# Two-layer mixer: the second layer's first two projection groups take activations before the norm

## The reference, cut to what matters

```python
shift, scale, gate = split(silu(c) @ w_ada + b_ada, 3)
h = x * rsqrt(mean(x * x) + eps) * norm_gain * (1 + scale) + shift
proj = h @ w_in                 # q, k, v, z of the attention, then q, k, v, z of the retention
```

## Time and profile before

| what | value |
|---|---|
| median of 3 runs | 1535.81 us (1535.54 to 1535.85) |
| time of the profiled execution | 1534.71 us |
| its span in the trace | 1533.0 us |
| TensorE busy, share of the span | 99% |
| DVE busy, share of the span | 74% |
| ACT busy, share of the span | 51% |
| mean granted TensorE clock | 0.997 |

### The profile page before, as it was taken

The page is one execution under the profiler, slowest core; times in us unless marked ns, Lnnn a source line. Parts: engine busy times, 40 slices in busy tenths (PEclk is TensorE's granted clock), DMA queues, the critical chain, the costliest instruction groups (busy, mean ns, idle before and its releaser), DMA issues.

```text
span 1533.0 us, 32039 instructions
## 1 busy us (share of the span) xinstructions
PE 1520.6 (99%) x12566; PEld 1480.7 (97%) x12566; DVE 1134.8 (74%) x1371; ACT 778.1 (51%) x930; POOL 35.4 (2%) x64
## 2 busy tenths in 40 slices
PE   9999999999999999999999999999999999999997
PEld 8999998999999999999999999999999989999997
DVE  7877777658988878878788887879854644764754
ACT  7645456545554445444444444445554643454544
POOL 0000001000000000000000000000000000000000
PEclk9999999999999999999999999999999999999998
DMA  9574566457876867767677776866475554455451
GB/s 351 168 272 159 203 191 246 155 173 265 311 291 239 299 222 274 260 237 285 238 272 240 260 272 223 297 228 210 147 251 194 193 192 165 154 162 179 164 180 56
DMA packets 86412, 340.31 MB, mean 222 GB/s; under 512 B 9896, under 2 KB 10424, under 8 KB 79808
## 3 DMA queue, kind: packets, MB, share of 16 engines
q1 hardware_dynamic: 77760, 281.05, 52.9%
q0 software_dynamic: 7712, 55.63, 10.2%
q10 hardware_dynamic: 864, 2.53, 0.4%
HBM read 337.03 MB, written 2.14 MB: 221 GB/s over the span
## 4 chain that ended last, share of the span: by engine, by line
PE 94%; DVE 4%; ACT 1%; issue 1%; DMA 0%; SPq 0%; DVEq 0%; ACTq 0%
PE PS L1328 27%; PE PS L1330 27%; PE PS L1332 27%; PE PS L1377 3%; PE PS L1376 3%; PE PS L1374 3%; DVE wlo L696 1%; PE PS L1523 1%; PE PS L1544 1%; ACT whi L333 1%; DVE conv_acc L777 1%; DMA raw<-weights 0%; PE PS L1701 0%; PE PS L1506 0%; DVE EM L881 0%
## 5 line engine op out<-in xcount | busy, mean ns | idle before, releaser
L696 DVE TENSOR_TENSOR wlo<-raw,whi 128x1024 fp32r<-128x1024 f32 x528 | 642.8, 1222 | 337.0 <-ACT whi L333 333.6
L333 ACT ACTIVATE whi<-raw 128x1024 fp32r<-128x1024 f32 x528 | 557.4, 1059 | 640.2 <-PE PS L1332 571.0
L1328 PE MATMUL PS<-gh,whi 128*128 128x256 f32 x3096 | 863.4, 279 | 0.7 <-DVE wlo L696 0.4
L1330 PE MATMUL PS<-gl,whi 128*128 128x256 f32 x3096 | 856.1, 277 | 0.0
L1332 PE MATMUL PS<-gh,wlo 128*128 128x256 f32 x3096 | 856.1, 277 | 0.0
L1328 PEld LDWEIGHTS PS<-gh,whi 128*128 128x128 f32 x3096 | 581.7, 188 | 5.6 <-issue 2.4
L1330 PEld LDWEIGHTS PS<-gl,whi 128*128 128x128 f32 x3096 | 581.4, 188 | 0.8
L1332 PEld LDWEIGHTS PS<-gh,wlo 128*128 128x128 f32 x3096 | 581.6, 188 | 0.0
L1328 PE MATMUL PS<-ah,whi 128*128 128x256 f32 x688 | 189.9, 276 | 0.0
L1330 PE MATMUL PS<-al,whi 128*128 128x256 f32 x688 | 189.9, 276 | 0.0
L1332 PE MATMUL PS<-ah,wlo 128*128 128x256 f32 x688 | 189.9, 276 | 0.0
(11 more groups left out here) (254 smaller groups left out, 892.9 us busy)
## 6 DMA issues: line engine op xcount, KB each, us to landing
raw<-weights SPq DMA_DIRECT2D x528, 512.0 KB, 3.5
ada_w<-w_ada POOLq DMA_DIRECT2D x48, 1024.0 KB, 6.5
EM<-rows POOLq DMA_DIRECT2D x1, 3072.0 KB, 12.4
X<-xT SPq DMA_DIRECT2D x3, 512.0 KB, 8.2
c<-const ACTq DMA_DIRECT2D x1, 1536.0 KB, 6.9
c_act<-c_rows POOLq DMA_DIRECT2D x1, 1024.0 KB, 6.7
KF<-factors POOLq DMA_DIRECT2D x2, 512.0 KB, 6.6
outT<-X SPq DMA_DIRECT2D x2, 512.0 KB, 3.2
```

The costliest lines, as they stand in the source:

```text
L333: act.activation(whi[:, j % SPLIT, :], raw[:, j, :], ACT.Copy).then_inc(s_hi, 1)
L696: dve.tensor_tensor(wlo[:, j % SPLIT, :], raw[:, j, :], whi[:, j % SPLIT, :].bitcast(F32), ALU.subtract).then_inc(s_lo, 1)
L1328: pe.matmul(out[:, t, :], whi[:, b, w], hi[:, kt, :], start=first and half == 0 and (apart or t % 2 == 0), stop=False, skip_group_check=True)
L1330: pe.matmul(out[:, t, :], whi[:, b, w], lo[:, kt, :], start=False, stop=False, skip_group_check=True)
```

## The change

Groups 0 and 1 of the second layer's input projection (the columns of z of the attention) take `gh`/`gl` made of X times gain and scale alone, without the norm factor and without the shift. The factor, one number for each position, is multiplied in by DVE when the two accumulators are emptied (`gate_scaled`), and the shift's part, `shift @ w_in` for these 1024 columns, is added as the bias of the silu. From group 2 on the projection takes the normed and shifted activations, which replace the first ones in `gh`/`gl` during group 1. The group d = 3 becomes an ordinary one; `last_pair`, `column_squares`, the spread and `idle` stay only at the end of the kernel (`last_pair`, `column_squares`) and in the first layer. The sum of squares is taken with `sum_squares` (one matmul with ones, in TensorE's slot 5), its root on ACT and its inverse on DVE in their slots 5.

The shift's part is made by DVE during `ffn`: after iteration 2 it adds the bias to the 16 sums, POOL writes them to memory and reads them back onto every partition (`s_rowb`), and in iterations 3 to 10 DVE multiplies this row with one row block of the transposed weights (`w_rowb`, 1 MB, loaded from ACT's queue) and sums it up. Iteration 2 is written out too.

```diff
         @block.gpsimd
-            with pool.Fori(1, ADA_TILES // 2) as i:
...
+            modulation_rows(1, 9)
+            pool.wait_ge(s_shift, 1)
+            pool.dma_start(shift, shift_col).then_inc(s_shiftd, 16)
+            pool.wait_ge(s_shiftd, 16)
+            pool.dma_start(s_rowb[:, :], shift.rearrange("p t -> (p t)").unsqueeze(0).to_broadcast([P, D])
+                           ).then_inc(s_shiftb, 16)
+            modulation_rows(9, ADA_TILES // 2)
...
         @block.scalar   (in ffn, at its top)
+                if i is not first and i is not second:
+                    act.wait_ge(s_wsum, i - 2)
+                    act.dma_start(w_rowb[:, :], w_shift[bass.ds(i - 3, 1), :, :].rearrange("a p n -> (a p) n")
+                                  ).then_inc(s_wrow, 16)
...
             for d in range(4):
+                split(B_IN2 - 1, LEAD + 2 * d)
+                split(B_IN2 - 1, LEAD + 2 * d + 1)
+                act.wait_ge(s_evac, G_IN2 - 4 + d + 3)
+                if d == 0:
+                    act.wait_ge(s_mt, 1)
+                if d < 2:
+                    squares(2, d, SQX2)
+                for t in range(4 * d, 4 * d + 4):
+                    early_hi(t)               # gh[t] = X[t] * modT[16 + t]
             def slot2(n):
+                if n in (0, 2):
+                    squares(2, 2 + n // 2, SQX2)
+                if n == 5:
+                    root(2, D)
+                if n == 8:
+                    act.wait_ge(s_wsum, 1 + 8)
+                    act.dma_start(c2[:, :, :, :], const2).then_inc(s_c2, 16)
+                if 9 <= n < 9 + DT // 2:
+                    late_hi(2 * (n - 9))
+                    late_hi(2 * (n - 9) + 1)
+                if n in (17, 18):             # silu with bias=shift_out[:, t], tile by tile
...
         @block.vector   (in ffn, third block)
+                    if j == 0 and i is not first and i is not second:
+                        shift_product(i)      # waits s_wrow; w_rowb *= s_rowb, summed into small[280 + i - 3]
                     taps = 0 if i is last else 2
...
             ffn(first)
-            with dve.Fori(2, last) as i:
+            ffn(second)
+            dve.wait_ge(s_ada, 16)
+            dve.tensor_tensor(shift_col, modT[:, 0:16], col("b_ada", 0, 16), ALU.add).then_inc(s_shift, 1)
+            dve.wait_ge(s_shiftb, 16)
+            with dve.Fori(3, last) as i:
...
+            for d in range(4):
                 split(B_IN2 - 1, LEAD + 2 * d)
                 split(B_IN2 - 1, LEAD + 2 * d + 1)
                 add_to_x(8 * (B_IN2 - 1) + 2 * d + 1, G_IN2 - 4 + d, (G_IN2 - 4 + d) % 2, 4 * d)
+                if d == 0:
+                    dve.wait_ge(s_mt, 1)
+                if d < 2:
+                    for t in range(4 * d, 4 * d + 4):
+                        early_lo(t)           # gl[t] = X[t] * modT[16 + t] - gh[t]
+                if d == 2:
+                    sum_chunk(2, 1, SQX2)
             def slot2(n):
+                if n < 4:
+                    early_lo(8 + 2 * n)
+                    early_lo(8 + 2 * n + 1)
+                if n in (1, 3):
+                    sum_chunk(2, 2 + n // 2, SQX2)
+                if n == 3:
+                    fold(2, 3, SQX2)
+                if n == 5:
+                    inverse_root(2)
+                    dve.wait_ge(s_rb, 3)
+                if n in (7, 15):
+                    gate_scaled(n // 8)
+                if 6 <= n < 6 + DT // 2:
+                    normed(2 * (n - 6))       # TH[t] = X[t] * modT[16 + t] * rb
+                    normed(2 * (n - 6) + 1)
+                if 9 <= n < 9 + DT // 2:
+                    late_lo(2 * (n - 9))      # gl[t] = TH[t] + modT[t] - gh[t]
+                    late_lo(2 * (n - 9) + 1)
...
             for n in range(IN2_SLOTS):
-                if n >= len(TURNS) - 2:
-                    split(B_IN2, LEAD + n)
+                split(B_IN2, LEAD + n)
                 slot2(n)
...
         @block.tensor
-            last_pair(2, range(4), True, 8 * B_IN2 - 2, ah2, al2)
-            column_squares(2, SQX2)
             def slot2(n):
-                if n == 6:
-                    idle(2)
+                if n == 5:
+                    sum_squares(2, SQX2)      # waits for fold(2, 3)
...
+            need = {0: lambda kt: early + kt + 1, 2: lambda kt: late + kt + 1}
```

More of the change, by code:

```diff
@@ L177, in build, with near_tile @@
         own = PS[:, 4:8, 0:S]
[L178 to L190, removed]
+        rcol = small[:, 228:230]
+        SQUARES, SUMS = (0, 4, 8, 12), (0, 3, 6, 9)
+        late_par = (G_OUT2 + 3) % 2
+        last_spread = PS[:, 2 * late_par + 1, 0:S]
+        shift_col, shift_out = small[:, 288:304], small[:, 280:288]
+        def near_tile(t):
+            return SQX4[:, 1, t, :]
         def seen(h, c):
@@ L307, in _, with modulation_rows @@
                 pool.dma_start(ada_w[:, b, :], w_ada[b, :, :]).then_inc(s_adaw[b], 16)
[L308 to L312 removed]
+            def modulation_rows(first, end):
+                with pool.Fori(first, end) as i:
+                    for b in range(2):
+                        pool.wait_ge(s_ada, i * 2 + (b - 1))
+                        pool.dma_start(ada_w[:, b, :], w_ada[bass.ds(i * 2 + b, 1), :, :].rearrange("a p n -> (a p) n")
+                                       ).then_inc(s_adaw[b], 16)
+            modulation_rows(1, 9)
[5 more added lines that the diff above has]
+            modulation_rows(9, ADA_TILES // 2)
             pool.wait_ge(s_gain, 4)
@@ L597, in ffn @@
                         ffn_hi(i, ah2)
-            first, last = 1, FF_GROUPS - 1
+            first, second, last = 1, 2, FF_GROUPS - 1
             ffn(first)
-            with act.Fori(2, last) as i:
+            ffn(second)
+            with act.Fori(3, last) as i:
                 ffn(i)
             ffn(last)
[L604 to L614, removed]
@@ new lines, in slot2 @@
+            def slot2(n):
+                if n in (0, 2):
[9 more added lines that the diff above has]
+                if n in (17, 18):
+                    act.wait_ge(s_evac, G_IN2 + 2 + 2)
+                    for t in range(4 * (n - 17), 4 * (n - 17) + 4):
+                        z = QB[:, ZA2 + t, :]
+                        ins = act.activation(z, z, ACT.Silu, bias=shift_out[:, t:t + 1])
+                    ins.then_inc(s_zs, 1)
@@ L1111, in _, with shift_product @@
             ffn_evac(8 * B_FF + 15, G_FF + 1, (G_FF + 1) % 2, UV)
-            first, last = 1, FF_GROUPS - 1
+            first, second, last = 1, 2, FF_GROUPS - 1
+            def shift_product(i):
+                dve.wait_ge(s_wrow, i * 16 - 32)
+                dve.scalar_tensor_tensor(w_rowb[:, :], w_rowb[:, :], 1.0, s_rowb[:, :], ALU.mult, ALU.mult,
+                                         accum_out=small[:, bass.ds(i + (280 - 3), 1)]).then_inc(s_wsum, 1)
             def ada_tile(i, k):
@@ L1351, in product_first @@
                                        skip_group_check=True)
-                mm.then_inc(s_used, 1)
-            def product_high_first(out, need):
-                for kt in range(2):
-                    pe.wait_ge(s_gh, 2 * DT + 6 + kt + 1)
-                    for w, x in ((whi, gh), (wlo, gh), (whi, gl)):
-                        if x is gl:
-                            pe.wait_ge(s_gl, need(kt))
-                        for t in range(4):
-                            at = 512 * kt + P * t
-                            mm = pe.matmul(out[:, t, :], w[:, 0, at:at + P], x[:, kt, :],
-                                           start=kt == 0 and w is whi and x is gh and t % 2 == 0, stop=False,
-                                           skip_group_check=True)
                 mm.then_inc(s_used, 1)
@@ L1453, in stream_in @@
                     return
-                if blk == B_IN2 and n == 0:
-                    product_high_first(acc_tiles(grp % 2), need)
-                    return
                 product(n % SPLIT, acc_tiles((grp + g) % 2), (2 * u, 2 * u + 1), u == 0, u == 7, gh, gl,
-                        ready=need if g == 0 else None)
+                        ready=need[g] if g in need else None)
             def stream_out(blk, grp, s, base, last=False):
@@ L1667, in down @@
                 pe.wait_ge(s_al, i + 1)
-                for d in range(4 if hi is ah else 3):
+                for d in range(4):
                     group(unit + 2 * d, 2 * d, 2, grp + d, (G_FF + d) % 2, hi, lo, None)
@@ L1801 @@
     factors = nc.dram_tensor("factors", (2, 4, 2, S), F32, kind="Internal").ap()
-    build(nc, *args, rows, factors, outT)
+    shift = nc.dram_tensor("shift", (P, DT), F32, kind="Internal").ap()
+    build(nc, *args, rows, factors, shift, outT)
     r = run_bass_kernel_spmd(nc, [arrays], core_ids=[0])
```

177 lines of the change are left out of this document (76 added, 101 removed).

## The result

The changed kernel takes 1543.43 us (median of 6 runs, 1540.79 to 1544.81), the one before 1535.67 beside it: ratio 1.0049 [1.0038, 1.0059], slower by some 7.5 us. The prediction was 1539.6, range 1534.0 to 1545.0, slower. The ratios leave out executions more than 1.5% above the quickest of the same kernel, here one of the kernel before at 1561.88; the medians keep them, and the last experiment profiles long executions of the changed kernel. The profiled execution of the changed kernel is the slowest of its six, with a span of 1542.9 against 1533.0.

What follows compares the result with a forecast made beforehand. TensorE, in flight 99% of the span, was taken as the bound, with only 7.1 us between the layers to win. 3.2 + 1.05 - 0.5 = +3.75 on the median 1535.81 gave 1539.6 us, range 1534.0 to 1545.0.

Steps and rivals of the forecast that it cites:

- the five waits: TensorE's predicted waits: 3.2 behind ffn(2), 1.05 at the last down block, 0.15, 1.75 and 4.2 between the layers.
- case A: The whole kernel as summed, 1539.6, with bounds 1536.8 to 1544.5; chance 0.42.
- Part 1: After ffn(2): the shift's one trip through memory takes 9.1, so TensorE waits 3.2 (1.6 to 6.7).
- rival C: After ffn(2): the shift's trip is quick because weight loads stop; wait 1.6, 1538.0, or 1536.4 if hidden; chance 0.15.
- Part 2: Iterations 3 to 10: one more product each, seven cost nothing, the one in iteration 10 loses 1.05 (0.9 to 1.3).
- Part 3: Between the layers: waits of 0.15, 1.75 and 4.2 plus 0.5 for the sum, 6.6 against 7.1: 0.5 won.
- the old trace's clock is kept: Between the layers: assumption that the clock stays as in the trace of the kernel before.
- Part 4: Group 1: DVE's work of 30.5 us fits in 12 units, 32.6 us, so nothing is lost.
- B: Clock falls to 1.2 GHz in the wait after ffn(2) or in slot 5: +6.35, 1542.2; chance 0.26.
- twice, 1544.8: The time if the clock falls in both long waits, after ffn(2) and in slot 5, at 2.6 each.
- E: Quick shift trip after ffn(2) and sum of squares not late between the layers, together: -3.95, 1531.9; chance 0.07.
- D: Between the layers: sum of squares isn't late if the fold is done by 1109.0; 6.6 won, 1533.5; chance 0.10.

Runs made afterwards that it cites:

- the last experiment: The changed kernel, unaltered, profiled three more times, one run each: 1543.7, 1561.27 and 1567.11 us.
- E1: Against the changed kernel, DVE's wait for the shift moved from ahead of the loop to the first product that uses its rows: 1538.75 us.
- E5: Changed kernel with DVE's wait at the first product, the product in the gate block and the sum of squares two slots later: 1530.88 us.
- E7: Changed kernel with both moves of the shift's path (DVE's wait at the first product, product in the gate block), between the layers unaltered: 1536.66 us.
- E3: Against the changed kernel, eight idle matmuls put into TensorE's wait for the folded sum of squares in slot 5: 1546.81 us.
- E8: The changed kernel, unaltered, profiled once more: 1543.7 us (one run).
- E4: Against the changed kernel, sum of squares, root, inverse, normed tiles and late splits put two slots later: 1538.63 us.
- E9: The changed kernel, unaltered, a second additional profile: 1561.27 us (one run).
- E6: E5 with ACT making the next two splits before a quarter's square and tiles, DVE's low tiles a quarter later: 1529.07 us.
- E2: Against the changed kernel, only the product with the shift moved from the down block's first split to the gate block's fifth: 1543.94 us.
- E10: The changed kernel, unaltered, a third additional profile: 1567.11 us (one run).

## Why the prediction held, and where its sum failed

The sign, the places and four of the five waits came as predicted; the time is 3.8 above the forecast, inside the range. The forecast itself, case A, has the clock kept, and the clock fell. That the median lies inside A's bounds (to 1544.5) all the same is luck: those bounds stand for slow transfers, not for the clock. By its steps:

- **Part 1**, 3.2 (1.6 to 6.7): 3.5, E1 shows it. The trip of 9.1 was 9.44, out of two errors that cancel. POOL went on 4.08 after its first issue, where the first layer's 8 KB took 1.97. These 8 KB go in 128 pieces, and beside weight loads (429 GB/s from 551.7 to 553; none from 211 to 212 in the first layer); no run parts the two reasons. The 1 MB came back in 4.8, not 6.5, while nothing else was moved; in E1, where DVE goes on and weight loads keep coming, it took 6.7 (E5 6.5, E7 7.8). That was rival C's reason, and these rows bear it out. By the Trainium skill, page "DMA: Bandwidth & Descriptors", section on the anatomy of a DMA on the GpSimd path, the two would take an estimated 2.0 and 4.4. The second is near the 4.8, the first is off by 1.8 from the 3.8 in which it landed.
- **Part 2**, 1.05: 1.9 in this profile, a term mis-sized. That iterations 3 to 9 cost nothing is right (456.95 in both). In iteration 10 `al` came 1.08 later, as summed. But I did not see that the addition of d = 0 would be late first, and matmuls behind a break may start 0.118 apart, as this stretch did: 0.7 in breaks and 1.2 that no wait shows. The 1.2 is partly chance: E1, E3 and E8, with the same late `al`, have the stage 1.3 to 1.4 longer than before the change, and E5 has 0.8 with `al` in time. E1 less E7, by the medians of runs under 1560, is 1.4.
- **Part 3**, 0.5 won: the chain of additions, splits and tiles was priced well. The wait of 0.15 did not appear; 1.75 became 1.0 (1.2 between matmuls), and 4.2 became 3.9. What failed is the sentence "the old trace's clock is kept": 1.4 more. E7, which has this part's cost alone, stands at +1.3 where 0.5 were to be won.
- **Part 4**, nothing: right; no wait of TensorE lies in group 1 or at the start of group 2, nor with the sum two slots later (E4, E5).
- **Rivals.** B is what happened, twice in four of the six runs by their mean clock. I gave it 0.26, with small matmuls that had kept the clock as the reason against it; there TensorE was doing something, here nothing. Priced at 2.6 for each fall, it measured 3.0 and 1.4 (1.7 and 2.5 in E8); that "twice, 1544.8" is the profiled execution's 1544.81 is a coincidence, since B stands on the median and has 5.2 for the clock where 4.4 was measured. The rule of the Trainium skill, page "TensorE: Matmul & The Clock Gate", section on the clock gate, that the clock falls after idleness, agrees with 13 of 14 waits, and E3 agrees too; E9's first wait does not. C's and E's quick trip did not come. D's condition did not hold, but E6 makes it hold, and its 6.6 is what is won.

In the span: 3.75 forecast, +4.4 for the clock, +0.85 for part 2, +0.4 for part 1's wait, -0.8 for shorter waits in part 3, and +1.2 ahead of the feed-forward loop and at the end, where the change does nothing (E3 and E2, with the same code there, have 393.94 and 394.93 in the first of these): 9.8 of 9.9.

So the idea was sound, and its placing took more than it gave: a wait placed ahead of work that it did not concern (E1), a product put where iteration 10 has no slack (E2), and a sum asked for two slots before it could be there (E4). Mended, it wins 6.3 us.

## What to carry to other kernels

Put a wait on a slow transfer where its data are used, not ahead of the queue's other work. Price a wait of TensorE of some 3 us with the clock behind it (here 1.4 to 3.0 more where it fell), and ask for a result only when the slower engine's in-order chain can have it, counted in TensorE's slots. Where a total does not resolve an edit, compare the stage that it touches.

## What was not expected of the hardware

TensorE's stream of these matmuls has two spacings at the same granted clock of 1.00: 0.113 (885 in 100 us) and 0.118 (852). It changes where the stream is broken, by a wait, by other matmuls or by one late start (0.05 late in E10, 0.03 in E5), and holds until a later break, over 34 us in the changed kernel, 528 in E4 and nearly 700 in E10. E4's 17.9 us and the executions of 1561 and 1567 come from it. The kernel before has the wide one too, between the layers from 1095.6 to 1109.6; its own executions near 1562 were not profiled. What decides which spacing follows stays open: behind a wait of 1.0 the stream became narrow in the changed kernel, behind 0.2 it stayed wide, and behind E9's 3.1 it became wide; E6 has the same small late start as E5 and stayed narrow.
